# All of w_down as split products, with the one-hot rows of the next experts built on GpSimd

## What is computed

```python
def moe_ffn(h, w_router, router_bias, w_gate, w_up, w_down, ws_gate, ws_up, ws_down):
    gates = route(h.reshape(B * S, D), w_router, router_bias).reshape(B, S, N_EXPERTS)
    def per_seq(args):
        hs, gs = args
        g = jnp.einsum('sd,edf->sef', hs, w_gate)
        u = jnp.einsum('sd,edf->sef', hs, w_up)
        act = jax.nn.silu(g) * u * gs[:, :, None]
        return jnp.einsum('sef,efd->sd', act, w_down)
    routed = lax.map(per_seq, (h, gates))
    shared = (jax.nn.silu(h @ ws_gate) * (h @ ws_up)) @ ws_down
    return routed + shared
```

## Time and profile before

| | us |
|---|---|
| median of 3 runs | 1070.29 |
| lowest and highest | 1069.88, 1074.86 |
| profiled execution, whole time | 1075.07 |
| profiled execution, span from first to last instruction | 1073.0 |

### The profile page before, as it was taken

One profiled execution on the slowest core, in us unless ns is written; L12 is line 12 of the kernel. 1 busy time (PEld: TensorE's weight loads), 2 busy tenths in 40 slices (PEclk: granted clock), 3 DMA queues, 4 the chain that ended last, 5 costly groups with the idle time before them and its releaser, 6 DMA issues.

```text
span 1073.0 us, 15239 instructions
## 1 busy us (share of the span) xinstructions
PE 1019.2 (95%) x4652; PEld 743.2 (69%) x4652; DVE 870.5 (81%) x1416; ACT 644.7 (60%) x743; POOL 299.5 (28%) x224
## 2 busy tenths in 40 slices
PE   4998999999998999999999999999999999999957
PEld 0786776557754777777777777777777777777723
DVE  1669766654768899999998989999999999999785
ACT  5334135643343678777777767777777777777511
POOL 1232221440303433323322323322322332332200
PEclk9899999999999999999999999999999999999979
DMA  9667743112254799999999999999999999999993
GB/s 338 260 244 266 257 174 99 59 40 89 102 212 145 283 376 367 365 378 386 391 382 378 355 365 359 378 374 383 371 373 343 362 335 336 346 358 359 360 412 119
DMA packets 71080, 318.67 MB, mean 297 GB/s; under 512 B 17232, under 2 KB 17744, under 8 KB 44560
## 3 DMA queue, kind: packets, MB, share of 16 engines
q1 hardware_dynamic: 36816, 200.30, 49.3%
q10 hardware_dynamic: 11616, 72.66, 17.9%
q0 software_dynamic: 22624, 45.40, 11.4%
HBM read 317.25 MB, written 39.85 MB: 333 GB/s over the span
## 4 chain that ended last, share of the span: by engine, by line
PE 80%; DMA 9%; DVE 7%; ACT 2%; issue 1%; ACTq 0%; SPq 0%; POOL 0%; DVEq 0%; POOLq 0%
PE ps L1348 11%; PE ps L1350 11%; PE ps L1349 11%; PE ps L1366 10%; PE ps L1033 8%; PE ps L1372 8%; PE ps L1123 6%; DMA hg<-h_rows,idxg 6%; PE ps L1442 3%; PE ps L1225 2%; DMA yr<-y_rows 2%; PE ps L1207 2%; PE ps L1049 2%; PE ps L1174 1%; PE ps L1285 1%
## 5 line engine op out<-in xcount | busy, mean ns | idle before, releaser
L1821 DVE TENSOR_TENSOR wlo<-raw,whi 128x2048 fp32r<-128x2048 f32 x136 | 305.2, 2285 | 0.0
L891 ACT ACTIVATE whi<-raw 128x2048 fp32r<-128x2048 f32 x136 | 261.4, 1923 | 0.0
L1348 PE MATMUL ps<-whi,hthi 128*128 128x512 f32 x544 | 225.1, 414 | 0.0
L1350 PE MATMUL ps<-whi,htlo 128*128 128x512 f32 x544 | 213.8, 393 | 0.0
L1349 PE MATMUL ps<-wlo,hthi 128*128 128x512 f32 x544 | 212.5, 391 | 0.0
L661 POOL DMA_INDIRECT y_rows<-ysb,idxs x68 | 69.0, 1015 | 444.9 <-DVE idxg L1816 389.6
L934 ACT ACTIVATE ysb<-ps 128x1024 f32<-128x1024 f32 x68 | 69.6, 1024 | 175.4 <-PE ps L1372 175.4
L653 POOL DMA_INDIRECT hg<-h_rows,idxg x70 | 140.3, 2005 | 71.0 <-DVE idxg L1816 50.5
L1366 PE MATMUL ps<-rawd,actt 128*128 128x512 f32 x272 | 127.8, 592 | 2.2 <-ACT actt L927 2.2
L1350 PEld LDWEIGHTS ps<-whi,htlo 128*128 128x128 f32 x544 | 102.1, 188 | 23.0
L1349 PEld LDWEIGHTS ps<-wlo,hthi 128*128 128x128 f32 x544 | 102.9, 189 | 17.6
(11 more groups left out here) (272 smaller groups left out, 1611.7 us busy)
## 6 DMA issues: line engine op xcount, KB each, us to landing
raw<-in_w_gate_dram SPq DMA_DIRECT2D x68, 1024.0 KB, 10.9
raw<-in_w_up_dram SPq DMA_DIRECT2D x68, 1024.0 KB, 12.9
rawd<-in_w_down_dram ACTq DMA_DIRECT2D x66, 1024.0 KB, 10.1
ada<-in_w_ada_dram SPq DMA_DIRECT2D x24, 1024.0 KB, 8.3
yr<-y_rows SPq DMA_DIRECT2D x6, 2048.0 KB, 19.3
wraw<-in_w_in_dram POOLq DMA_DIRECT2D x8, 1024.0 KB, 5.7
woraw<-in_w_out_dram SPq DMA_DIRECT2D x16, 256.0 KB, 3.0
yr<-y_rows SPq DMA_DIRECT2D x8, 512.0 KB, 11.7
```

The lines of the kernel that those rows point to most:

```text
L891: A(whi[:, s, m_, :], raw[:, s, m_, :], ACT.Copy).then_inc(hi_ok, 1)
L1348: mm(out_, hthi[s][:, k, :], hi, start=(k == 0), stop=False)
L1350: ins = mm(out_, htlo[s][:, k, :], hi, start=False, stop=(k == KD - 1))
L1821: V.tensor_tensor(wlo[s][:, m_, :], raw[:, s, m_, :], whi[:, s, m_, :].bitcast(F32), ALU.subtract).then_inc(lo_dve, 1)
```

## The change

The second half of w_down is split too. ScalarE makes the two high halves one after the other (`down_high`), VectorE the two low halves (`down_low`), and TensorE multiplies twelve fast matmuls in place of six fast ones and two float32 ones (`down`). The two buffers `wdhi` held the high part of the first half for each slot; now they hold the two halves of one block. The one-hot rows leave VectorE: GpSimd copies their columns (into `vcur` and the new `pcur`) and makes the four comparisons, behind its gather. At the end of the block loop `y_out(last, 0)` stands ahead of `down_high(last, 1)`. The loops of VectorE and GpSimd are cut where the tables of the last eight experts shift, a matter of addresses only.

```diff
+            def onehot(i, s, shift):
+                b = num(i, s) + shift
+                gp.wait_ge(idx_mm, num(i, s))
+                gp.sem_inc(onehot_go, 1)
...
+                gp.tensor_copy(vcur[:, :, :], src)
...
+                gp.tensor_copy(pcur[:, :], pcol.rearrange("p t b -> p (t b)")).then_inc(pcur_ok, 1)
+                gp.wait_ge(pcur_ok, num(i, s) - 4)
+                gp.sem_inc(onehot_go, 1)
+                for t in range(TT):
+                    ins = gp.tensor_scalar(s_onehot[:, t, :], iotab[:, :], pcur[:, t:t + 1], None, ALU.is_equal)
+                ins.then_inc(onehot_ok, 1)
...
                 gather(*after(i, s, 2))
+                if ahead:
+                    onehot(*after(i, s, 3), shift)
...
             def down_high(i, s):
                 ac.wait_ge(wd_in[s], i * 16 + 16)
-                A(wdhi[s][:, :, :], rawd[:, s, :, 0:DC], ACT.Copy).then_inc(wdhi_ok, 1)
+                for hf in range(2):
+                    A(wdhi[hf][:, :, :], rawd[:, s, :, hf * DC:(hf + 1) * DC], ACT.Copy).then_inc(wdhi_ok, 1)
...
             silu(last, 1)
+            y_out(last, 0)
             down_high(last, 1)
-            y_out(last, 0)
...
             def down(i, s):
-                pe.wait_ge(wd_in[s], i * 16 + 16)
-                pe.wait_ge(actt_ok, num(i, s) + 1)
+                pe.wait_ge(actl_ok, num(i, s) + 1)
                 if not (isinstance(i, int) and num(i, s) == 0):
                     pe.wait_ge(y_ok, num(i, s))
-                for k in range(KF):
-                    mm(bank(5), actt[:, k, :], rawd[:, s, k, DC:D], start=(k == 0), stop=(k == KF - 1))
-                pe.wait_ge(wdlo_ok, num(i, s) + 1)
...
+                for hf in range(2):
+                    pe.wait_ge(wdlo_ok, num(i, s) * 2 + (hf + 1))
+                    for k in range(KF):
+                        hi, lo = wdhi[hf][:, k, :], wdlo[:, s, k, hf * DC:(hf + 1) * DC]
+                        mm(bank(4 + hf), acth[:, k, :], hi, start=(k == 0), stop=False)
+                        mm(bank(4 + hf), acth[:, k, :], lo, start=False, stop=False)
+                        ins = mm(bank(4 + hf), actl[:, k, :], hi, start=False, stop=(k == KF - 1))
                 ins.then_inc(dn_mm, 1)
...
             def down_low(i, s):
-                v.wait_ge(wdhi_ok, num(i, s) + 1)
-                V.tensor_tensor(wdlo[:, s, :, 0:DC], rawd[:, s, :, 0:DC], wdhi[s][:, :, :].bitcast(F32), ALU.subtract)\
-                 .then_inc(wdlo_ok, 1)
+                for hf in range(2):
+                    cols = slice(hf * DC, (hf + 1) * DC)
+                    v.wait_ge(wdhi_ok, num(i, s) * 2 + (hf + 1))
+                    V.tensor_tensor(wdlo[:, s, :, cols], rawd[:, s, :, cols], wdhi[hf][:, :, :].bitcast(F32),
+                                    ALU.subtract).then_inc(wdlo_ok, 1)
...
-                onehot(*after(i, s, 3), shift)
                 if late >= 2:
                     act_low(*after(i, s, -2))
```

More of the change, by code:

```diff
@@ L216, in block_kernel @@
         vcur = small("vcur", [P, TT, VC], BF16)
+        pcur = small("pcur", [P, TT], F32)
         destr = at("destr", [P, COLS], I32, 187 * KB)
@@ L324, in block_kernel @@
         onehot_ok = sem("onehot_ok")
+        onehot_go = sem("onehot_go")
+        pcur_ok = sem("pcur_ok")
         idx_mm = sem("idx_mm")
@@ L663, in scatter, with step_pool @@
                                       bounds_check=last_routed, oob_is_err=False).then_inc(scattered[s], 16)
-            def step_pool(i, s, late=True):
+            def onehot(i, s, shift):
+                b = num(i, s) + shift
+                gp.wait_ge(idx_mm, num(i, s))
+                gp.sem_inc(onehot_go, 1)
+                src = vtab[:, :, b, :] if isinstance(b, int) else \
+                    vtab[:, :, bass.ds(b, 1), :].rearrange("p t b v -> p t (b v)")
+                gp.tensor_copy(vcur[:, :, :], src)
+                pcol = posb[:, :, b:b + 1] if isinstance(b, int) else posb[:, :, bass.ds(b, 1)]
+                gp.tensor_copy(pcur[:, :], pcol.rearrange("p t b -> p (t b)")).then_inc(pcur_ok, 1)
[4 more added lines that the diff above has]
+                ins.then_inc(onehot_ok, 1)
+            def step_pool(i, s, late=True, ahead=True, shift=0):
                 if late:
@@ L679, in _ @@
             gather(1, 0)
-            step_pool(0, 1, late=False)
+            step_pool(0, 1, late=False, ahead=False)
             step_pool(1, 0, late=False)
@@ L700, in _ @@
             step_pool(1, 1)
-            with gp.Fori(2, E // 2) as i:
+            with gp.Fori(2, MID // 2 - 2) as i:
                 for s in range(SLOTS):
                     step_pool(i, s)
-            with gp.If(m > 0):
-                with gp.Fori(E // 2, m + E // 2) as i:
-                    for s in range(SLOTS):
-                        step_pool(i, s)
+            for b in range(MID - 4, MID):
+                step_pool(b // 2, b % 2, shift=LASTE if b + 3 >= MID else 0)
+            with gp.Fori(MID // 2, m + E // 2) as i:
+                for s in range(SLOTS):
+                    step_pool(i, s, shift=LASTE)
             scatter(m + (E // 2 - 2), 1)
@@ L1360, in down @@
             def down(i, s):
-                pe.wait_ge(wd_in[s], i * 16 + 16)
-                pe.wait_ge(actt_ok, num(i, s) + 1)
+                pe.wait_ge(actl_ok, num(i, s) + 1)
                 if not (isinstance(i, int) and num(i, s) == 0):
                     pe.wait_ge(y_ok, num(i, s))
-                for k in range(KF):
-                    mm(bank(5), actt[:, k, :], rawd[:, s, k, DC:D], start=(k == 0), stop=(k == KF - 1))
-                pe.wait_ge(wdlo_ok, num(i, s) + 1)
-                pe.wait_ge(actl_ok, num(i, s) + 1)
-                for k in range(KF):
-                    for j, (a_, w) in enumerate(((acth, wdhi[s][:, k, :]), (acth, wdlo[:, s, k, 0:DC]),
-                                                 (actl, wdhi[s][:, k, :]))):
-                        ins = mm(bank(4), a_[:, k, :], w, start=(k == 0 and j == 0), stop=(k == KF - 1 and j == 2))
+                for hf in range(2):
[5 more added lines that the diff above has]
+                        ins = mm(bank(4 + hf), actl[:, k, :], hi, start=False, stop=(k == KF - 1))
                 ins.then_inc(dn_mm, 1)
@@ L1791, in col, with onehot @@
                 return tile[:, bass.ds(b, 1)]
-            def onehot(i, s, shift=0):
-                b = num(i, s) + shift
+            def onehot(i, s):
+                b = num(i, s)
                 src = vtab[:, :, b, :] if isinstance(b, int) else \
@@ L1851, in act_low, with step_dve @@
                  .then_inc(actl_ok, 1)
-            def step_dve(i, s, late=3, shift=0):
+            def step_dve(i, s, late=3):
                 if late >= 3:
@@ L1891, in _ @@
             v.wait_ge(fill_ok, 1)
-            with v.Fori(3, MID // 2 - 2) as i:
+            with v.Fori(3, E // 2) as i:
                 for s in range(SLOTS):
                     step_dve(i, s)
-            for b in range(MID - 4, MID):
-                step_dve(b // 2, b % 2, shift=LASTE if b + 3 >= MID else 0)
             m = v.value_load(npair[0:1, 0:1], min_val=0, max_val=OVER // 2)
-            with v.Fori(MID // 2, m + E // 2) as i:
-                for s in range(SLOTS):
-                    step_dve(i, s, shift=LASTE)
+            with v.If(m > 0):
+                with v.Fori(E // 2, m + E // 2) as i:
+                    for s in range(SLOTS):
+                        step_dve(i, s)
             last = m + (E // 2 - 1)
```

## The result

| | us |
|---|---|
| median before (4 runs) | 1071.4 (1069.88 to 1074.86) |
| median of the change (4 runs) | 1168.25 (1166.32 to 1170.78) |
| ratio, 95% interval | 1.0909, 1.0883 to 1.0935 |
| forecast | 1105, range 1076 to 1128 |
| span of the profiled execution, before and after | 1073.0, 1167.0 |

The change costs 97 us where 34 were forecast. The end of the program costs nothing: from the start of the chain's longest piece there, the reading back of result rows, to the end of the span it is 57.5 us before and 55.3 in the change (its piece starts at 1111.70). The whole difference is in the block loop. The copies of the result rows (`ysb`) start 58 beats apart between 430.2 and 1093.0, a beat of 11.43 us against 9.91 to 9.94 before.

The account below looks back on a forecast made before the run. TensorE set the 9.91 us beat, with a loop through TensorE, ScalarE and VectorE only 0.59 us behind. Beat 10.45: 63 x (10.45 - 9.91) = 34 us, plus 1, gave 1105 us, range 1076 to 1128.

Parts of the forecast that it names:

- The end of the program: After the block loop: one more high and low half of w_down's last block, counted as 1 us.
- What would show it: Signs listed for the block loop: 10.45 us beat, TensorE idle for comparisons, two comparisons of about 2.2 us, two short.
- ScalarE's part: Second high half of w_down stands ahead of `acth`: 0.95 us more, so `acth` ends at 6.62 instead of 5.67.
- the shorter down product: On TensorE, six more fast matmuls replace the float32 half: 1.72 - 1.40 = 0.32 us less a block.
- The third and fourth: GpSimd's last two comparisons run after VectorE's low parts end at 11.49, 0.55 us together; one-hot rows ready at 12.04.
- one to a seam: A GpSimd instruction reading SBUF gets through only between two VectorE subtractions with two SBUF inputs, one each time.
- the hold-ups at the seams: VectorE delayed by passing comparisons between its subtractions: 0.1 us at each of two places.
- the way from the last comparison to gate/up: TensorE's start after the one-hot rows: 0.23 us of waking and 0.2 us for the index matmuls.
- All four comparisons left over: Upper bound if GpSimd's copies miss the gap: two blocks take 21.4 us or more, a beat of 10.7 us.
- the two-block loop: Down matmul, ScalarE, VectorE, gate/up matmul, down matmul again: 19.83 us over two blocks, 0.59 us to spare before the change.
- The loop alone: Rival: GpSimd finishes in time, only the ScalarE and VectorE delays count; beat 10.05 us, 1079 us, chance 0.12.
- The mutual lock: Rival: comparisons hold VectorE up for their full length too; beat 11.2 us, 1150, or 1130 for half; chance 0.18.

## Why the prediction was right and wrong

**Right: the sign and most parts of the mechanism.** GpSimd's small instructions are shut out by VectorE's subtractions, and TensorE idles ahead of the index matmuls for the comparisons, as "What would show it" had it. ScalarE's part came as worked out: `acth` ends 6.62 us after the start of the last down matmul (from 702.40 to 709.02), the prediction's 6.62. From the first gate/up matmul to the last down matmul it is 8.30 us (from 705.36 to 713.66), forecast 8.38; the shorter down product is there, and nothing of it reaches the time. The end of the program played no part, and the DMA engines had room.

**Wrong: the size, by one term.** The step that failed is the sentence "The third and fourth have no seam left before 11.49. They run after it, 0.55 us together". The comparisons end 2.14 us after the low parts (from 714.45 to 716.59) in nearly half of the blocks and 1.69 in the mean, not 0.55. It has two errors. A comparison costs 0.59 us, not 0.29: the price was taken from the nearest row with 128 elements, another operation. And the rule "one to a seam" was carried from a copy and a sum to comparisons with a column operand, whatever their start. The first ahead of the pair and the second at its seam, as the prediction placed them, is what 16 of 57 blocks show; in 27 the first lasted through both low parts, so that all four were left over, not two. Even in the 16 blocks the term is 1.04 us.

Worked out for the block shown, with 0 at its last down matmul (702.40): gate/up starts at 716.87, which is 14.47, where the prediction had 12.67. Of these 1.8 us the comparisons make 2.14 - 0.55 = 1.59. The low parts end at 12.05 and not at 11.49, 0.56 more, because VectorE's step itself had waited for the index matmuls. Less than forecast are the hold-ups at the seams (0.2 us, here none; 0.10 us in 23 of 59 blocks) and the way from the last comparison to gate/up (0.28 us, not 0.43).

**Wrong: the loop.** That wait is the sign of a loop that the prediction did not draw: index matmuls, tables, VectorE's step, low parts, comparisons, index matmuls. It spans one block, so each microsecond in it costs a whole one in each block. The experiment with two comparisons more shows it (1.18 us a block for 1.18 us). That VectorE's tables wait for the index matmuls had no place in the prediction's sum. The two errors belong together: with 0.55 us for the comparisons this loop would take 11.39 - 2.14 + 0.55 = 9.80 us (an estimate from the loop above), less than the 10.5 forecast, and would not have counted. With 2.14 it binds.

**The bounds.** "All four comparisons left over" was named as the bound on the dear side, but at 0.29 us each and in the two-block loop, 10.7 us. At 0.59 us each it would have been 11.49 + 2.36 + 0.43 + 8.38 = 22.66 us for two blocks, 11.33 for one, about 1161 us: close to the result and still under it. The case was right, the price and the loop were not. An operation that no row shows should have had a wide range; GpSimd's 128x512 elements of another operation took 1.3 us and more in the kernel before.

**The rivals.** The loop alone had a beat of 10.05 us, and once the wait is taken away 10.01 is measured. That agreement is at least in part luck, since easing the two-block loop further gained nothing. The mutual lock gave the numbers nearest to the result (1130 to 1150), for a reason that the traces refute; and the "half of it" is a slip, since half of its 79 us gives 1110 and not 1130.

## What to carry to other kernels

Work moved from a busy engine to an idle one is free only if nobody waits for it: the same six instructions cost 54 us alone and 97 together with the split where TensorE waits for them in the same step, 13 us (split included) with one more buffer and one block more lead, and nothing where nobody waits. Before moving a step, write down the loop that it closes (who waits for it, and what it waits for), count the blocks that the loop spans, and put the price of the new engine into it, with the blocked time behind the other engine's longest instructions. A small GpSimd instruction beside a VectorE that subtracts SBUF tensors nearly all the time took as long as one of those subtractions, or as two, whatever its own length.

## What the runs showed of the hardware that was not expected

- A comparison of 128 bf16 elements per partition with a column as scalar takes 0.59 us on GpSimd, 0.52 us with a constant; VectorE takes 0.74 us for four.
- A comparison with a column that begins after the first of two back-to-back VectorE subtractions of 2048 elements waits for the end of both (4.56 us in 51 of 51 blocks, up to 4.89). With a constant it ends behind the first (2.37 us in 50 of 50). With a column and begun ahead of the pair it also gets in at the seam.
- VectorE loses 0.10 us of a subtraction at such a seam (2.38 against 2.28 us), 0.14 us where a comparison is still running at its start (2.42), at most 0.25 (2.53), and nothing where none meets it: 2279 ns in the kernel with comparisons nobody waits for, 2285 in before.
- TensorE's lower granted clock in the loop of waits (0.95 to 0.97; 0.957 over the whole execution) cost nothing: at 1.00 in the loop the time was the same, 1170.05 against 1168.25 us.
